# The first mixer's output projection, spread by channel group over the passes of the next groups

## The reference, cut to what matters

```
proj = h @ w_in                       # z, x, B, C, dt
xBC  = silu(causal_dwconv(x,B,C) + b) # 4 taps
y    = ssd(x, dt, A, B, C)            # recurrence over chunks of 128 tokens
y    = (y + D*x) * silu(z)            # 2048 channels, 4 groups of 512
y    = y * rsqrt(mean(y*y over the 512 channels of a group) + eps) * norm_w
x    = x + y @ w_out                  # 2048 -> 1024, fp32, residual
```

## Time and profile before

| | us |
|---|---|
| median of three runs (1002.44 to 1006.59) | 1005.31 |
| the profiled execution's own time | 1002.74 |
| its span | 1001.0 |
| PE busy | 911.0 (91%) |
| DVE busy | 661.3 (66%) |
| ACT busy | 482.3 (48%) |
| POOL busy | 161.5 (16%) |

### The profile page before, as it was taken

One profiled execution on the slowest core, in us unless ns is written; L12 is line 12 of the kernel. 1 busy time (PEld: TensorE's weight loads), 2 busy tenths in 40 slices (PEclk: granted clock), 3 DMA queues, 4 the chain that ended last, 5 costly groups with the idle time before them and its releaser, 6 DMA issues.

```text
span 1001.0 us, 20427 instructions
## 1 busy us (share of the span) xinstructions
PE 911.0 (91%) x7371; PEld 891.3 (89%) x7371; DVE 661.3 (66%) x1040; ACT 482.3 (48%) x897; POOL 161.5 (16%) x101
## 2 busy tenths in 40 slices
PE   6889699978878896599999999999999999989996
PEld 5689698968878896499999999999999999989996
DVE  4679998997899899975464645445555444554533
ACT  5467647655765576653444433233233233333344
POOL 6302451352137124500000000000000000000000
PEclk7989798979998897699999999999999999999999
DMA  7136546443654354313231433232223332222222
GB/s 196 46 93 185 140 122 170 129 134 111 183 158 134 95 181 140 100 49 101 86 103 43 127 90 99 85 103 84 84 84 93 98 102 84 84 84 85 84 61 85
DMA packets 158835, 108.02 MB, mean 108 GB/s; under 512 B 5024, under 2 KB 146876, under 8 KB 158204
## 3 DMA queue, kind: packets, MB, share of 16 engines
q1 hardware_dynamic: 119780, 76.15, 25.9%
q10 hardware_dynamic: 38592, 30.54, 10.2%
q0 software_dynamic: 400, 0.55, 0.3%
HBM read 95.35 MB, written 12.14 MB: 107 GB/s over the span
## 4 chain that ended last, share of the span: by engine, by line
PE 60%; DVE 20%; issue 7%; ACT 5%; DVEq 1%; ACTq 0%; POOL 0%; POOLq 0%
PE bank L1256 39%; PE bank L1415 18%; DVE acc L897 5%; DVE wlo L791 4%; DVE zh L972 3%; DVE st L961 1%; DVE hs L928 1%; DVE xd L911 1%; ACT em L571 1%; ACT thx L548 1%; PE bank L1317 1%; DVE dtx L955 1%; DVE yr L965 1%; PE bank L1326 1%; DVE yob L945 1%
## 5 line engine op out<-in xcount | busy, mean ns | idle before, releaser
L1256 PE MATMUL bank<-hhi,whi 128*128 128x260 f32 x1664 | 342.9, 288 | 10.9 <-ACT ext L538 10.0
L1256 PE MATMUL bank<-hhi,wlo 128*128 128x260 f32 x1664 | 339.1, 286 | 0.0
L1256 PE MATMUL bank<-hlo,whi 128*128 128x260 f32 x1664 | 339.0, 286 | 0.0
L1256 PEld LDWEIGHTS bank<-hhi,whi 128*128 128x128 f32 x1664 | 261.0, 192 | 14.9 <-ACT ext L538 11.6
L461 ACT ACTIVATE whi<-raw 128x1024 fp32r<-128x1024 f32 x136 | 143.8, 1057 | 253.8 <-PE bank L1256 154.1
L1256 PEld LDWEIGHTS bank<-hlo,whi 128*128 128x128 f32 x1664 | 260.8, 192 | 0.0
L1256 PEld LDWEIGHTS bank<-hhi,wlo 128*128 128x128 f32 x1664 | 260.7, 191 | 0.0
L791 DVE TENSOR_TENSOR wlo<-raw,whi 128x1024 fp32r<-128x1024 f32 x132 | 169.9, 1287 | 41.1 <-ACT whi L461 39.2
L1415 PE MATMUL bank<-hhi,whi 128*128 128x260 f32 x512 | 104.6, 286 | 4.1 <-DVE hlo L1074 4.1
L1415 PE MATMUL bank<-hlo,whi 128*128 128x260 f32 x512 | 103.9, 285 | 0.0
L1415 PE MATMUL bank<-hhi,wlo 128*128 128x260 f32 x512 | 103.6, 284 | 0.0
(11 more groups left out here) (213 smaller groups left out, 984.5 us busy)
## 6 DMA issues: line engine op xcount, KB each, us to landing
raw<-in_sc_w_in SPq DMA_DIRECT2D x64, 512.0 KB, 4.0
raw<-in_ssd_w_in SPq DMA_DIRECT2D x40, 512.0 KB, 3.9
abc<-a_rows ACTq DMA_DIRECT2D x16, 512.0 KB, 4.6
st<-in_state_ssm ACTq DMA_DIRECT2D x16, 512.0 KB, 4.8
out_new_ssm_s<-st ACTq DMA_DIRECT2D x16, 512.0 KB, 3.7
raw<-in_ssd_w_out SPq DMA_DIRECT2D x16, 512.0 KB, 3.8
raw<-in_sc_w_out SPq DMA_DIRECT2D x16, 512.0 KB, 3.8
bcbc<-bc_rows ACTq DMA_DIRECT2D x4, 1024.0 KB, 7.7
```

The source lines that it names most:

```text
L1256: mm = pe.matmul(b[:, 0:TH], w[:, slot, k * P:(k + 1) * P], h[:, k, cols], start=(k == 0 and i == 0), stop=(k == KT - 1 and i == 2))
```

## The change

The output projection of group g-1 is done inside the pass of group g. The loop over groups is unrolled and each group gets its own order of chunks; an output chunk `o0..o3` holds the weights of the group's 4 tiles of y by 256 output channels, and makes two results (`part` 0 and 1), so it takes two turns of the bank pairs. Chunks o2 and o3 of group 2 and all four of group 3 come at the end. In all there are still 16 output chunks of 48 matmuls.

```diff
-ORDER = ["B", "C", "x0", "x1", "x2", "x3", "z0", "z1", "z2", "z3"]
+FIRST = ["B", "C", "x0", "x1", "x2", "x3", "z0", "z1", "z2", "z3"]
+MIDDLE = ["B", "C", "x0", "x1", "x2", "o0", "x3", "o1", "z0", "o2", "z1", "o3", "z2", "z3"]
+LAST = ["B", "C", "x0", "x1", "x2", "o0", "x3", "o1", "z0", "z1", "z2", "z3", "o2", "o3"]
+AFTER = ["o0", "o1", "o2", "o3"]
+LAYER0 = [(g, what) for g, order in enumerate((FIRST, MIDDLE, MIDDLE, LAST, AFTER)) for what in order]
+NUMBER = {chunk: n for n, chunk in enumerate(LAYER0)}
+PAIR = {}
+for _g, _what in LAYER0:
+    for _part in range(2 if _what[0] == "o" else 1):
+        PAIR[_g, _what, _part] = (len(PAIR) % 2, len(PAIR) // 2)
...
+            def out_chunk(g, c):
+                n = NUMBER[g, f"o{c}"]
...
+                for part in range(2):
+                    p, turn = PAIR[g, f"o{c}", part]
+                    pe.wait_ge(pair_free[p], turn + 1)
+                    for k in range(STEPS):
+                        pe.wait_ge(yg_hi, (g - 1) * STEPS + k + 1)
+                        pe.wait_ge(yg_lo, (g - 1) * STEPS + k + 1)
...
+                    mm.then_inc(proj_done if part else half_done, 1)
...
+                    def proj(what):
+                        p, turn = PAIR[g, what, 0]
+                        pe.wait_ge(pair_free[p], turn + 1)
...
 
...
+            def residual0(g, c, part):
+                p, turn = PAIR[g, f"o{c}", part]
...
+                dve.tensor_tensor(xT[:, k, 0:TH], xT[:, k, 0:TH], bank[2 * p][:, 0:TH], ALU.add)
+                dve.tensor_tensor(xT[:, k, TH:T], xT[:, k, TH:T], bank[2 * p + 1][:, 0:TH], ALU.add).then_inc(pair_free[p], 1)
```

```
# TensorE, the pass of a group
                    proj("B"); proj("C")
+                    if g > 0: group_sums(g - 1)
                     proj("x0"); proj("x1"); group_matrices(); turn(0)
                     proj("x2")
+                    if g > 0: out_chunk(g, 0)
                     within(0); turn(1)
                     proj("x3"); across(0); within(1); turn(2)
+                    if g > 0: out_chunk(g, 1)
                     proj("z0"); across(1)
+                    if 0 < g < 3: out_chunk(g, 2)
                     proj("z1"); within(2)
+                    if 0 < g < 3: out_chunk(g, 3)
                     proj("z2"); turn(3); across(2); within(3); proj("z3"); across(3)
...
+            out_chunk(3, 2)
...
             group_sums(3)
+            out_chunk(3, 3)
+            for c in range(4):
+                out_chunk(4, c)
# VectorE, the pass of a group
                     conv(0); silu(0); next_low(B); conv(1); silu(1); next_low(C)
+                    if g > 0: norm_scale(g - 1, 0..3)
                     conv(2); silu(2); next_low(x0)
+                    if g > 0: y_low(g - 1, 0..3)
                     CBm; bcd; causal(0); weigh_dt(0); conv(3); silu(3); next_low(x1)
                     recur(0); skip(0); weigh_dt(1); sample_x(0); conv(4)
+                    if g > 0: residual0(g, 0, 0)
                     causal(1); silu(4)
+                    if g > 0: residual0(g, 0, 1)
                     next_low(x2)
+                    if g > 0: next_low(o0)
                     add_earlier(0); recur(1); conv(5); skip(1); sample_add(0)
                     weigh_dt(2); sample_x(1); silu(5); next_low(x3)
+                    if g > 0: residual0(g, 1, 0)
                     causal(2)
+                    if g > 0: residual0(g, 1, 1); next_low(o1)
                     sample_out(0); add_earlier(1); sample_add(1); next_low(z0); silu_z(0)
+                    if 0 < g < 3: residual0(g, 2, 0)
                     recur(2); skip(2)
+                    if 0 < g < 3: residual0(g, 2, 1); next_low(o2)
                     sample_x(2); gate(0); next_low(z1); silu_z(1)
-                    weigh_dt(3); sample_out(1)
+                    if 0 < g < 3: residual0(g, 3, 0)
+                    sample_out(1)
+                    if 0 < g < 3: residual0(g, 3, 1); next_low(o3)
+                    weigh_dt(3)
                     causal(3); gate(1); add_earlier(2); ...
# ScalarE, in a group with g > 0
                     tanh_conv(1)
+                    act.wait_ge(stat_mm, g); logs(group_parts(g - 1), ...); roots(group_parts(g - 1), ...)
                     evac_conv(2)
+                    y_high(g - 1, 0..3)
                     segments(0); tanh_conv(2)
...
```

More of the change, by code:

```diff
@@ L260, in _ @@
             sp.dma_start(dwr[:, :, :], w_in0[:, :, DI + XBC:DI + XBC + HEADS]).then_inc(dtw_in, 16)
[L261 to L272, removed]
+            for n, (g, what) in enumerate(LAYER0):
+                if what[0] == "o":
+                    c = int(what[1])
+                    load(n, n, w_out0[:, (g - 1) * STEPS:g * STEPS, c * 256:(c + 1) * 256])
+                else:
+                    if what == "B":
+                        col = 2 * DI + g * NS
+                    elif what == "C":
+                        col = 2 * DI + (GROUPS + g) * NS
+                    else:
+                        col = (g * STEPS + int(what[1])) * P + (DI if what[0] == "x" else 0)
+                    load(n, n, w_in0[:, :, col:col + P])
             def load_out(base, w):
@@ L371, in _ @@
             pool.wait_ge(sqs_zero, 1)
-            with pool.Fori(0, GROUPS // 2) as G:
-                for gg in range(2):
-                    g = group_half(G, gg)
+            for g in range(GROUPS):
+                if True:
                     def weigh(q):
@@ L432, in _ @@
             act.sem_inc(hi_done, SLOT)
-            act.sem_inc(proj_free, 2)
+            for p in range(2):
+                act.sem_inc(pair_free[p], 1)
             act.sem_inc(fin_st, 16)
@@ L711, in out_phase @@
-                    if layer == 1 and r == 1:
+                    if r == 1:
                         act.wait_ge(tail_t, 2)
@@ L1109, in add_square @@
+            residual0(3, 2, 1)
+            next_low(3, "o2")
+            residual0(3, 3, 0)
+            for q in range(STEPS):
+                norm_scale(3, q)
+            residual0(3, 3, 1)
+            next_low(3, "o3")
+            for q in range(STEPS):
+                y_low(3, q)
             def add_square(layer, k):
@@ L1176, in _ @@
                     low(j * 4 + (IN1 + 3 + SLOT), 3)
-            out_phase(OUT1, 1)
+            with dve.Fori(0, STEPS) as J:
+                block1(J, 0)
+            for b in range(2):
+                dve.wait_ge(st_st[b], 16 * 9)
+            with dve.Fori(0, STEPS) as J:
+                block1(J, 1)
+            out_phase(OUT1)
             dve.wait_ge(col_rms, 1)
@@ new lines, in group_sums @@
+            def group_sums(g):
+                pe.wait_ge(sqs_done, STEPS * (g + 1) + 1)
+                pe.wait_ge(yd_done, 8 * (g + 1) + 1)
+                pe.wait_ge(yo_done, STEPS * (g + 1) + 1)
+                for half in range(2):
+                    mm = pe.matmul(bank[6 + half][:, 0:TH], ones[:, :], sqs[:, g, half * TH:(half + 1) * TH], start=True, stop=True)
+                mm.then_inc(stat_mm, 1)
+            for g in range(GROUPS):
+                if True:
+                    def proj(what):
+                        n = NUMBER[g, what]
+                        p, turn = PAIR[g, what, 0]
+                        pe.wait_ge(pair_free[p], turn + 1)
+                        if n == 0:
```

509 lines of the change are left out of this document (285 added, 224 removed).

## The result

The changed kernel takes 1050.86 us, the median of four runs (1050.48 to 1055.21), against 1005.17 for the kernel before on the same chip. The ratio is 1.0468, with a 95% interval of 1.0447 to 1.0490. Its profiled execution took 1050.48 us, with a span of 1048.8. The forecast was 1054.

A forecast was written before the change was run, and what follows sets the result against it. It took VectorE to bound the passes. Added work and S1 to S7, less the loop step, gave +106 us and the shorter end -57: +49 on 1002.7, then 2.6 for the median, 1054 us (range 1036 to 1073).

The forecast's parts named there:

- added work: VectorE's added norms, `y_low`, residuals and weight splits: 15.6 us per pass with four output chunks, 10.6 in group 3.
- S1: In a pass, VectorE waits at `norm_scale` for ScalarE's Ln and Exp with two table loads: 2.3 us.
- S2: Behind `conv(2)`, VectorE waits for ScalarE's copies, `segments` and tanh 2.9 us instead of 1.06: 1.8 more.
- S3: At `recur(0)`, VectorE waits while half of o0 and the chunk states run on TensorE: 3.7 us.
- S4: x3 waits for o0's residual after `conv(4)` to free its pair; VectorE then waits 3.3 us, slow clock start included.
- S5: z0 waits for o1's first residual; VectorE then waits at `add_earlier(1)`: 3.7 us with the slow start.
- S6: Groups 1 and 2: z1 waits for o2's first residual, and VectorE's next instruction, `recur(2)`, needs z1 and chunk states: 6.9 us.
- S7: Groups 1 and 2: o3 waits for o2's second residual, z2 follows, and VectorE waits for `weigh_dt(3)`: 4.7 us.
- The loop step: Unrolling the loop over groups takes back its one step on VectorE: 3.35 us.
- The end of the layer: From the last gate to the second layer, with four output chunks left: about 42 us, 57 us less than before.
- the one in which waits fall into slack: In the passes, TensorE's answers come as early as now and S3 to S7 vanish: 999 us, chance 0.07.
- The rival in which GpSimd's stretching gives back 27.7 us: GpSimd's work falls into the new stops, giving back half of S3 to S7: 1026 us, chance 0.15 for 1010 to 1036.

The follow-up runs named there:

- run 6: The kernel before with all five hardware loops over pairs of groups unrolled and nothing else changed: 995.99 us, ratio 0.9914 to the kernel before.
- run 7: run 4 with Ln, Exp and the norm one step later, behind x0's sums, evacuation and convolution work: 996.05 us, 0.9915.
- runs 1 to 4: The changed kernel with calls moved, all work kept: three new orders singly, then all together; 1041.38, 1037.38, 1033.59 and 1001.96 us.
- run 4: The changed kernel with early residuals of o0 and o1, chunk states ahead of o0, z1 and z2 ahead of o2 and o3: 1001.96 us, 0.9975.
- run 9: run 7 plus o2 and o3 of group 2 in the last pass, B's copy ahead of `y_high`, VectorE's end reordered: 990.39 us, 0.9852.
- run 1: The changed kernel with the first residuals of o0 and o1 earlier on VectorE: 1041.38 us, 1.0372 to the kernel before.
- run 5: The changed kernel with each output chunk inside a pass cut from 48 matmuls to 4, other work kept: 1048.18 us, 1.0434.
- runs 2 and 3: The changed kernel with `within(0)` and `turn(1)` ahead of o0 (1037.38 us); separately, with z1 ahead of o2 and z2 ahead of o3 (1033.59 us).

## Why the prediction was right

The mechanism and the places held; the sum held too, but partly because two errors in it cancel. Term by term, in us of VectorE's waiting or work per pass:

| term | predicted | group 1 | group 2 | group 3 |
|---|---|---|---|---|
| added work | 15.6 (10.6) | 15.0 | 16.3 | 9.7 |
| S1 Ln and Exp | 2.3 | 2.35 | 2.35 | 2.34 |
| S2 ScalarE behind them (wait less 1.06) | 1.8 | 1.44 | 1.44 | 1.45 |
| S3 `recur(0)` | 3.7 | 3.56 | 3.55 | 3.56 |
| S4 `add_earlier(0)` | 3.3 | 3.62 | 3.91 | 3.13 |
| S5 `add_earlier(1)` | 3.7 | 4.13 | 4.32 | 3.91 |
| S6 `recur(2)` behind z1 | 6.9 (none) | 6.98 | 7.00 | 0.21 |
| S7 up to `weigh_dt(3)` | 4.7 (none) | 6.29 | 4.85 | 1.02 |

- **Work.** Added busy time is 40.9 us in the three passes, 41.8 predicted. The added instructions took no longer than their means before (2.77 us for four `norm_scale`, 3.1 predicted). But the 40.9 is a net figure: unrolling alone makes the busy time 6.4 us longer (run 6), and against run 6 only 34.5 us are added.
- **S1 and S2.** The wait for Ln and Exp is there with both table loads in it; run 7 took 0.8 of the 2.35 us of S1 and all of S2. ScalarE in group 1:

```profile
153.03 1.28 ACT L460 ACT_TABLE_LOAD   x1
155.19 1.28 ACT L466 ACT_TABLE_LOAD   x1
156.49 0.73 ACT L466 ACTIVATE sqs<-sqs 128x260 f32<-128x260 f32 x2
```

- **S3 to S6** were the heart of the forecast, and runs 1 to 4 show the cause of each. S3 goes when the chunk states stand ahead of o0. S4 and S5 go when the residuals come earlier. S6 goes when z1 stands ahead of o2. The slow start after a stop of TensorE, 1.4 us in the forecast, is there and is larger at x3: the chunk takes 8.4, 8.6 and 7.8 us in the three passes, and z0 7.4, 7.6 and 7.2, where 7.3 was taken for both from the earlier trace rows. That S4 is right all the same is luck: in group 1 VectorE needed 5.9 us from the freed pair to `add_earlier(0)`, not 4.8, since `causal(1)` took 2.33 and not 1.21.
- **S7** was the most undersized in group 1: 6.3 for 4.7, and 4.9 in group 2. The end of it, `weigh_dt(3)`, waits 3.86 both times, and small waits for o2's and o3's halves and a weight split come ahead of it, 2.4 us in group 1, which I had counted as cover.
- **A stop that the forecast lacks**, `sample_add(2)` behind GpSimd: 1.79 us in each pass, 5.4 in all. It stays in every one of the reordered kernels.
- **The loop step** was mis-sized the most in proportion. I gave back 3.35 us for unrolling, the one visible gap on VectorE. Run 6 shows 6.4 in the three passes: 12.8 us less idle time and 6.4 us more busy time. The sum goes thus: 40.9 us of net busy time, 71.4 of stops in the table, 5.4 at `sample_add(2)`, less 12.8 of idle time that unrolling removed, makes 104.9, where 103.3 was measured and 106 forecast. The stops came to 9 us more than the 67.6 forecast, and unrolling took back 9 us more of idle time than the 3.35. That the total fits so well is thus in good part luck.
- **The end of the layer** lasts 42.4 us, as predicted (42). The sums started 3.75 us after the last pass (3.2 predicted) and the first of group 3's output chunks 17.1 us after it (16.1). Its four chunks then took 25.3 us, where I had 26.
- **The second layer** moved by 1.1 us, counted at nothing.

Of the rivals, the one in which waits fall into slack (999 us) did not come true for this order. VectorE's idle time rose in each pass; the slack on TensorE was real but lay elsewhere. With the order of run 4 the same chunks give 1002, and with that of run 9 990. The Trainium skill (Perfetto Trace Analysis, Optimization Strategy) says that interleaving regimes with different most-contended engines may improve the time. In this kernel it cost 4.7% in the order as made, and in the best order found it gave 1.5%, of which the unrolled loops alone give 0.7 to 0.9. The rival in which GpSimd's stretching gives back 27.7 us is refuted in that size by VectorE's busy time: against the kernel before nothing is given back, and against run 6 no more than some 6 us. The Trainium skill (ScalarE: Activation LUTs, the section on table sets) says that Ln and Exp share a set and that a pair needs one load. The trace after does not agree: it has two, 1.28 us each, in every pass, and the wait is the 2.35 us that two loads give.

What stays open: why VectorE's busy time grew when the loops were unrolled, and again in run 1; and how much of run 5's missing gain is the lower clock, beyond the 2.3 us at one stop. The 1.64 us that VectorE still waits at `weigh_dt(3)` in group 1 of run 9 are no round trip: TensorE is busy 20.3 of the 20.7 us before it, at the full clock, so there it is simply full.

## What to carry to other kernels

Before work is moved under another stage's cover, list who hands back the buffer that it uses, and what that engine wants next. If the busiest engine frees a bank pair and its next instruction needs a result that is queued behind the refill of that pair, it pays for the whole refill each time, however idle the other engine looks. Here the same chunks gave +46 us in the order as made, -3 with three groups of calls moved and -14 with some more. Against the kernel before with its loops unrolled that is +55, +6 and -7. Adding up each round trip from the timeline placed the order as made, and runs 2 and 3, within some 3 us. It was off by 13 us in run 1, 12 in run 5, 6 in run 7 and 4 in run 4, where a stop that was taken away came back in part at the next place. Price an unrolled loop by itself first, since its gain can hide in a change that also moves work.

## What the runs showed of the hardware

- Taking a hardware loop away saved more than the step between iterations: the kernel takes 8.3 us less where the step is 3.35. In the loop a register operation of 57 ns stands on VectorE's sequencer ahead of each of the 72 taps, and three taps take 2.64 us; unrolled it is gone, and they take 2.42. One tap takes the same in both, 784 and 785 ns in the median.
- Taking 440 matmuls away left the passes at nearly the same length (380.7 us against 378.5), while the granted clock fell from 0.92, 0.90 and 0.91 to 0.81, 0.81 and 0.84 of 2.4 GHz. TensorE waited longer for VectorE, and in group 1 the first pair of matmuls behind each wait for `residual0` took 0.80 us. In the first two passes of run 9, where TensorE is idle 7.5 and 9.7 us, the clock is 0.95.
- What a stop of TensorE cost afterwards: behind 5.4 us of idle time the 48 matmuls of a chunk took 8.4 us at a granted clock of 0.66, against 5.83 at 1.00.
